# Overlapping the residual and norm boundaries of a two-block transformer kernel with the products on both sides, and moving two gate columns ahead of the attention

## What is computed

```python
# block 1
h = rmsnorm(x, g_pre_mix)
q, k, v, g, u, sv, a_ret, a_sgu = split(h @ w_in)
merged = sigmoid(a_ret) * retention(q, k, v, g) + sigmoid(a_sgu) * spatial_gating(u, sv)
x = x + rmsnorm(merged @ w_out, g_post_mix)                  # out1
h2 = rmsnorm(x, g_pre_ffn)                                   # read by up1
x = x + rmsnorm(conv_gated_mlp(h2, w_up, w_down), g_post_ffn)  # down1
# block 2
h = rmsnorm(x, attn_norm)                                    # h3, read by kv_iq
a_q, a_k, a_v, i_q, i_k, i_w, b_q, b_k, b_v, g_a, g_b = split(h @ w_in_2)
o_a = attention_on_the_128_best_keys(a_q, a_k, a_v, index(i_q, i_k, i_w))
o_b = sliding_window_attention(b_q, b_k, b_v, sinks)
mix = sigmoid(g_a) * (o_a @ w_branch_a) + sigmoid(g_b) * (o_b @ w_branch_b)
x = x + mix @ w_out_2                                        # out2
h2 = rmsnorm(x, mlp_norm)                                    # h4, read by up2
x = x + square(relu(h2 @ w_up_2)) @ w_down_2                 # down2
return rmsnorm(x, final_norm)
```

## Time and profile before

| | us |
|---|---|
| median of three runs | 1676.07 |
| profiled execution | 1677.33 |
| span of its instructions | 1675.5 |
| PE busy | 1620.2 |
| POOL busy | 799.6 |
| DVE busy | 774.1 |
| ACT busy | 491.4 |

### The profile page before, as it was taken

One profiled execution on the slowest core, in us unless ns is written; L12 is line 12 of the kernel. 1 busy time (PEld: TensorE's weight loads), 2 busy tenths in 40 slices (PEclk: granted clock), 3 DMA queues, 4 the chain that ended last, 5 costly groups with the idle time before them and its releaser, 6 DMA issues.

```text
span 1675.5 us, 19583 instructions
## 1 busy us (share of the span) xinstructions
PE 1620.2 (97%) x7556; PEld 1339.4 (80%) x7556; DVE 774.1 (46%) x1076; ACT 491.4 (29%) x735; POOL 799.6 (48%) x304
## 2 busy tenths in 40 slices
PE   7999999999998999999998999979999899999998
PEld 5887788888887888888886887867878788888886
DVE  6701588800555666664005488954452632013202
ACT  3012211200003434333123244245542343123312
POOL 5874287777876444444446003411135444434442
PEclk9999999999999999999998999989999999999999
DMA  5332033332233233332221322210022132232221
GB/s 201 101 126 75 3 105 101 101 101 84 92 101 101 76 101 100 99 90 93 95 101 59 99 79 72 80 51 26 26 76 101 52 99 101 101 101 95 89 97 72
DMA packets 123280, 147.47 MB, mean 88 GB/s; under 512 B 5142, under 2 KB 98374, under 8 KB 123206
## 3 DMA queue, kind: packets, MB, share of 16 engines
q1 hardware_dynamic: 121622, 141.90, 26.2%
q10 hardware_dynamic: 1584, 4.52, 0.8%
HBM read 144.31 MB, written 2.10 MB: 87 GB/s over the span
## 4 chain that ended last, share of the span: by engine, by line
PE 87%; DVE 7%; POOL 3%; issue 1%; ACT 1%; DMA 0%; SPq 0%; DVEq 0%; POOLq 0%; ACTq 0%
PE ps L582 26%; PE ps L583 26%; PE ps L584 26%; PE ps L691 2%; DVE work L1649 2%; PE ps L921 2%; PE ps L761 2%; DVE top L1646 2%; PE ps L907 2%; POOL w_lo L526 1%; DVE h_rows L1340 1%; POOL w_hi L517 1%; PE ps L818 1%; PE ps L749 1%; DMA raw<-in_w_in 0%
## 5 line engine op out<-in xcount | busy, mean ns | idle before, releaser
L526 POOL TENSOR_TENSOR w_lo<-raw,w_hi 128x1024 fp32r<-128x1024 f32 (+1 forms) x246 | 617.8, 2533 | 694.4 <-ACT w_hi L965 690.9
L582 PE MATMUL ps<-hT_hi,w_hi 128*128 128x512 f32 (+1 forms) x960 | 371.4, 387 | 1.0 <-DVE hT_lo L1351 0.5
L584 PE MATMUL ps<-hT_hi,w_lo 128*128 128x512 f32 (+1 forms) x960 | 368.2, 384 | 0.0
L583 PE MATMUL ps<-hT_lo,w_hi 128*128 128x512 f32 (+1 forms) x960 | 368.2, 384 | 0.0
L517 POOL TENSOR_TENSOR w_hi<-raw,cells 128x2048 fp32r<-128x2048 f32 x45 | 168.2, 3739 | 158.9 <-PE ps L582 158.9
L965 ACT ACTIVATE w_hi<-raw 128x2048 fp32r<-128x2048 f32 (+1 forms) x85 | 161.0, 1895 | 247.9 <-PE ps L582 246.2
L582 PEld LDWEIGHTS ps<-hT_hi,w_hi 128*128 128x128 f32 x960 | 181.9, 189 | 36.8 <-POOL w_lo L526 1.4
L584 PEld LDWEIGHTS ps<-hT_hi,w_lo 128*128 128x128 f32 x960 | 181.7, 189 | 35.4
L583 PEld LDWEIGHTS ps<-hT_lo,w_hi 128*128 128x128 f32 x960 | 181.8, 189 | 34.3 <-issue 0.2
L583 PE MATMUL ps<-w_lo,f_hi 128*128 128x512 f32 x432 | 170.2, 394 | 0.0
L582 PE MATMUL ps<-w_hi,f_hi 128*128 128x512 f32 x432 | 169.3, 392 | 0.0
(11 more groups left out here) (258 smaller groups left out, 2128.7 us busy)
## 6 DMA issues: line engine op xcount, KB each, us to landing
raw<-in_w_in SPq DMA_DIRECT2D x86, 512.0 KB, 4.6
raw<-in_w_up SPq DMA_DIRECT2D x76, 512.0 KB, 4.5
raw<-in_w_down SPq DMA_DIRECT2D x54, 512.0 KB, 4.1
raw<-in_w_out SPq DMA_DIRECT2D x16, 512.0 KB, 4.1
raw<-in_w_ret_o SPq DMA_DIRECT2D x8, 512.0 KB, 4.5
raw<-in_w_sgu_o SPq DMA_DIRECT2D x8, 512.0 KB, 4.4
x<-in_x SPq DMA_DIRECT2D x4, 512.0 KB, 7.5
raw<-in_w_branch_b SPq DMA_DIRECT2D x4, 512.0 KB, 4.4
```

The costliest lines, as they stand in the source:

```text
L526: nc.gpsimd.tensor_tensor(w_lo[:, s, c], raw[:, s, c], w_hi[:, s, c].bitcast(f32), ALU.subtract).then_inc(unit_split, 1)
L582: first = nc.tensor.matmul(dst, a_hi, b_hi, start=start, stop=False)
L583: nc.tensor.matmul(dst, a_hi, b_lo, start=False, stop=False)
L584: return first, nc.tensor.matmul(dst, a_lo, b_hi, start=False, stop=stop)
```

## The change

1. **Joint last two units.** In out1, down1, out2 and down2_1 the last two units are worked together, tile by tile (`last_two_L`): each tile gets its 4 x 3 x 2 matmuls of both units and is then complete. After the first half of tiles 2 and 3 PE transposes tiles 0 and 1 of the next `h_rows`.
2. **Next stage.** `first_two_T` takes the place of `first_T`: the first two units (four columns) are worked for the first 256 tokens, then for the rest; tile 2 is transposed ahead of the second column and tile 3 ahead of the fourth. kv_iq works both its units tile by tile, tiles 2 and 3 transposed after its tiles 0 and 1. No keep-warm transposes there.
3. **Slots.** The first unit of each joint pair and the second unit of each next stage have spare slots in memory that is free then. `FREE` says which unit must have started before a hi is written.
4. **Who splits.** From out1 on ACT writes every hi. DVE writes the lo of the first two units after each boundary, ahead of the boundary's steps. POOL adds nothing to `x` any more; DVE adds all four tiles. `STEPS` is A0 B0 A1 C0 B1 A2 C1 B2 A3 C2 B3 C3.
5. **Tickets** are waited for in the new order in which PE completes them (`ORDER`).
6. **Attention.** `GA_IN` is 6: two more gate columns ahead of the attention, 8 parts instead of 16 inside it, at steps 2, 6, ... 30. `index_score(2)` and `(3)` run inside `select(1)`, after its rounds 4 and 10.
7. ACT's loop over up2 is written out instead of looped.

```diff
-GA_IN = KT // 2
-PARTS = [2 + 2 * n for n in range(16)] + [46 + 3 * n // 2 for n in range(16)]
+GA_IN = 6
+GA_PARTS = 4 * (KT - GA_IN)
+PARTS = [2 + 4 * n for n in range(GA_PARTS)] + [46 + 3 * n // 2 for n in range(16)]
...
-GIVEN = [0, *range(U0["up1"] + 2, U0["kv_iq"]), *range(U0["iq_ik"], U0["up2_0"]), *range(U0["up2_0"] + 2, N_UNITS)]
+GIVEN = [0, *range(U0["out1"], N_UNITS)]
+JOINT = {phase: U0[phase] + n - 2 for phase, n in (("out1", 4), ("down1", FB // 2), ("out2", 4), ("down2_1", 8))}
+NEXT = {"out1": "up1", "down1": "kv_iq", "out2": "up2_0"}
+def slot_tables():
+    slot, free = {u: u % 2 for u in range(N_UNITS)}, {u: u for u in range(N_UNITS)}
+    for phase, u in JOINT.items():
+        slot[u], slot[u + 1] = (phase, 0), u % 2
+        free[u], free[u + 1] = u - 1, u
+        if phase in NEXT:
+            slot[u + 2], slot[u + 3] = (u + 1) % 2, (phase, 1)
+            free[u + 2], free[u + 3], free[u + 4] = u + 1, u + 1, u + 3
+    return slot, free
...
+def completion_order():
+    order = list(range(N_TICKETS))
+    for phase, h in (("out1", "h2"), ("down1", "h3"), ("out2", "h4")):
+        o, h, k = T0[phase], T0[h], T0["kv_iq"]
+        after = [o, o + 1, o + 2, o + 3, o + 4, h, h + 1, o + 5, o + 6, h + 2, h + 3, o + 7]
+        if phase == "down1":
+            after += [k, h + 4, h + 5, k + 1, h + 6, h + 7, k + 2, k + 3]
+        for n, t in enumerate(after):
+            order[t] = o + n
+    return order
...
+            def first_two_T(u, t, phase):
                 for half in range(2):
                     for tt in (2 * half, 2 * half + 1):
                         await_h(phase, tt)
                     tok = slice(half * S // 2, (half + 1) * S // 2)
-                    for c in range(2):
+                    for c in range(4):
+                        hi, lo = weights(u + c // 2, KT, 256, wait=half == 0 and c % 2 == 0)
                         if half == 0:
-                            if c == 1:
-                                for tt in (2, 3):
-                                    h_transposes(phase, tt)
+                            if c % 2:
+                                h_transposes(phase, 2 + c // 2)
                             claim(t + c)
...
+            def last_two_L(u, t, k0, l_hi, l_lo, ready, phase):
+                both = [weights(u + j, 2, D, wait=j == 1) for j in range(2)]
+                for kk in range(4):
+                    ready(k0 + kk)
+                for tt in range(NT):
+                    tok = slice(tt * P, (tt + 1) * P)
+                    for half in range(2):
+                        cc = slice(half * 512, half * 512 + 512)
+                        for kk in range(4):
+                            hi, lo = both[kk // 2]
+                            first, last = three(bank(t + 2 * tt + half), l_hi[:, k0 + kk, tok], l_lo[:, k0 + kk, tok],
+                                                hi[:, kk % 2, cc], lo[:, kk % 2, cc], False, kk == 3)
+                            if tt == 0 and half == 0 and kk % 2 == 0:
+                                first.then_inc(unit_started, 1)
+                        last.then_inc(psum_ready, 1)
+                        if phase and half == 0 and tt >= 2:
+                            h_transposes(phase, tt - 2)
...
+            for u in range(JOINT["out1"], U0["up1"] + 2):
+                give_hi(u, started=True)
             boundary("norm", T0["out1"], T0["h2"])
+            give_hi(U0["up1"] + 2, started=True)
...
+            low(U0["up1"])
+            low(U0["up1"] + 1)
             boundary("norm", T0["out1"], T0["h2"], 0, 1)
...
-            for tt in range(1, NT):
-                select(tt)
+            select(1, between={4: 2, 10: 3})
+            select(2)
+            select(3)
```

More of the change, by code:

```diff
@@ L330, in two_blocks @@
         rms_made = sem("rms_made")
-        x_updated = sem("x_updated")
         x_added = sem("x_added")
@@ L551, in _ @@
             split(1)
-            split_all(2, U0["up1"] + 1)
-            boundary(T0["out1"])
-            split(U0["up1"] + 1, last=T0["h2"] - 1)
-            split_all(U0["up1"] + 2, U0["kv_iq"])
-            split(U0["kv_iq"])
-            boundary(T0["down1"])
-            split(U0["kv_iq"] + 1, last=T0["h3"] - 1)
-            pool.wait_ge(unit_split, 2 * (U0["kv_iq"] + 2))
+            split_all(2, U0["out1"])
+            for u in range(U0["out1"], U0["up1"]):
+                split(u)
+            split_all(U0["up1"] + 2, JOINT["down1"])
+            for u in range(JOINT["down1"], U0["kv_iq"]):
+                split(u)
+            await_psum(pool, T0["h3"] - 1)
             zeroed = Count(pool, pads_zeroed)
@@ L565, in _ @@
             zeroed.wait()
-            split_all(U0["g_b"] + 2, U0["up2_0"])
-            split_all(U0["up2_0"], U0["up2_0"] + 2)
-            split_all(U0["up2_0"] + 2, N_UNITS)
+            split_all(U0["g_b"] + 2, U0["out2"])
+            for u in range(U0["out2"], U0["up2_0"]):
+                split(u)
+            split_all(U0["up2_0"] + 2, JOINT["down2_1"])
+            for u in range(JOINT["down2_1"], N_UNITS):
+                split(u)
         @block.tensor
@@ L822, in gb_column @@
                 column(U0["g_b"] + c // 2, G_B[c], KT, 256, c % 2, hT_hi, hT_lo)
-            wide("kv_iq", after="h3")
+            both = []
+            for tt in range(NT):
+                await_h("h3", tt)
+                if tt == 0:
+                    both = [weights(U0["kv_iq"] + h, 4, 512) for h in range(2)]
+                t = T0["kv_iq"] + tt
+                claim(t)
+                tok = slice(tt * P, (tt + 1) * P)
+                for kk in range(KT):
+                    hi, lo = both[kk // 4]
+                    first, last = three(bank(t), hT_hi[:, kk, tok], hT_lo[:, kk, tok], hi[:, kk % 4, :],
+                                        lo[:, kk % 4, :], kk == 0, kk == KT - 1)
+                    if tt == 0 and kk % 4 == 0:
+                        first.then_inc(unit_started, 1)
+                last.then_inc(psum_ready, 1)
+                if tt < 2:
+                    h_transposes("h3", tt + 2)
             wide("iq_ik", IB_W)
@@ L973, in boundary @@
                 step.up(nc.scalar.activation(sq[:, 1:2], eps, ACT.Sqrt))
-                for which, tt in STEPS:
+                for which, tt in steps(kind):
                     tok = slice(tt * P, (tt + 1) * P)
@@ L1118, in _ @@
                 up_unit(j)
-            for u in range(U0["down1"] + 2, U0["kv_iq"]):
+            for u in range(U0["down1"] + 2, U0["kv_iq"] + 2):
                 give_hi(u, started=True)
```

149 lines of the change are left out of this document (82 added, 67 removed).

## The result

The changed kernel took 1632.21 us, the median of four runs (1631.12 to 1632.53), beside 1676.26 for the kernel before on the same chip: a ratio of 0.9735 with a 95% interval of 0.9723 to 0.9747, 44.1 us less. The forecast was 1633.0. The total is right to 0.8 us; of its two parts one is right and one is not, and a third thing, which the forecast didn't have, fills the gap.

What follows compares the result with a forecast made beforehand. PE, busy 97% of the span, bounds the kernel, so only its waits and slow-clock stretches can be won. Boundaries 34.6 plus attention 8.3 give 42.9 us, 1676.07 to 1633.0; own range 1630 to 1636.

Steps and rivals of the forecast that it cites:

- Boundaries: out1 to up1, down1 to kv_iq, out2 to up2_0: gains 12.2, 13.7 and 10.2 us, less 3 x 0.5 stall: 34.6 us.
- T+5.9: Start of ACT's square for tile 0, 5.9 us after the joint product's start T; tile 0 is complete at T+5.6.
- Rival A: Late chain to `h_rows` stalls PE inside the joint product: 4.5 us more, 1637.5; chance 0.17.
- First eight steps: Attention's start, 21.62 us before: falls to 10.0 without the 9.6 us bubble, 11.6 gained; 0.3 lost to DVE.
- DVE free at 1100.9: Before the attention: DVE done about when PE arrives (1101.0, old clock), a tie; 0.3 us taken, up to 4.
- gain of 4.3 us: Index scores 2 and 3 inside select(1) fill DVE's 3.91 us wait and some 0.4 more.
- Steps 8 to 32: Attention, 46.16 us before: 6 parts instead of 12 gain 8.2 us, less 1.5 for latency they had covered.
- Rival B: Attention becomes latency-bound, waits for `probs` and `probs_T` take 6 of 8.2 us: 4.5 more, 1637.5; chance 0.12.
- extra part at step 32: Attention: one more part gone at step 32, 1.2 us gained.
- Moved cells: Shifted buffer addresses, listed as free: no time gained or lost.
- Rival C: The joint product's second unit is late at the boundaries: 6 us more, 1639; chance 0.05.
- D: Slower than before: units of up1 and up2 each wait 1.5 us for weight splitting, 51 us, 1684; chance 0.02.

Runs made afterwards that it cites:

- after_back64: The changed kernel with the region that holds the stage operands (oT, yT, mT, f) starting 64 bytes lower, as in the kernel before: 1637.88 us.
- scores_plain: The changed kernel with index scores 2 and 3 ahead of the mask again, not inside the first selection: 1631.99 us.
- table_first: The changed kernel with the Sqrt table load ahead of ACT's hi copies at each of the three boundaries instead of behind them: 1630.28 us.
- scores_late: The changed kernel with index score 3 placed later in the first selection, after its last but one round instead of after the eleventh: 1630.78 us.

## Why the prediction was right, and where not

- **Boundaries, 34.6 us forecast, 33.5 measured.** The steps held: PE's waits for `h_rows` below 3 us, no keep-warm rows, clock 1.00 throughout, `h_rows` at 1.28 us for every tile. `h_rows` of 3.18 is gone, and POOL is idle from 491 to 532. POOL's memsets after h3 (883.60 to 885.86 in the changed kernel) ran beside the `h_rows` at 884.05, which took 1.29 us: an instruction that only writes did not stretch it, as forecast. From the joint start to the first unit of full width were 50.27, 47.97 and 48.70 us, where 48.9, 47.3 and 48.9 were forecast. At out1 the waits named in the rows are 1.45 us against the 0.5 taken; with 48.9 + 1.45 - 0.64 for the spacing, 0.56 are left that have no row of their own. The step that was mis-sized is the start of the chain: the square was put at T+5.9 and came at T+7.1, because the second unit's hi waited for its load (1.32 us, the DMA) and the table load stood behind it. The forecast had seen that load "just where A0 starts" and put 0 to 0.2 us on it; taking it away removed both waits.
- **Rival A** (4.5 us more) didn't come; the named waits at the three boundaries are 2.1 us, nearer to the 1.5 taken than to its 6.
- **First eight steps, 11.3 us forecast (11.6 less 0.3), 9.15 measured.** The step that failed is "DVE free at 1100.9"; it was 1105.5 by the same clock. Its gain of 4.3 us assumed that the scores take the same time wherever they stand. They fell on a POOL low. Measured, the gain is 0.1 (3.91 of wait less 3.85). PE waited 2.26 us instead of 0.3, and the clock, taken as restored, cost about 1.25; against that some 1.1 us of the stretch came out better than forecast, and were not traced.
- **Steps 8 to 32, 6.7 us forecast, 5.16 measured.** Six parts of 1.37 us were removed (8.2) and 3.0 came back, not 1.5. PE's idle time in the stretch rose from 1.56 us (46.16 - 44.60) to 3.58 (41.00 - 37.42), and cutting the same parts finer takes it to 0.83 (38.05 - 37.22) and the stretch down by 2.95. The comparison of busy times that the forecast used (ACT 1.0, DVE 0.8, PE 1.2 us a step) only says that no engine is over its load. The loss is latency: the chain logits, `probs`, transposes, `probs_T`, values runs over three engines, and where no product stands between, PE waits: 0.98 us at 1093.87, 0.98 at 1107.73 and 1.01 at 1121.62, once in eight steps, and less between. **Rival B** (6 lost) names the mechanism, at twice its size.
- **The extra part at step 32:** 0.78 measured, 1.2 forecast.
- **Spacing, nothing forecast, 7.1 measured.** "Moved cells" was listed under free. The forecast had both values in front of it, 0.227 and 0.233, and took them as properties of the products. It didn't ask why one 512-column matmul should cost 3% more than another.
- **Rival C and D:** no new wait for weights: PE's waits for POOL's lows are 1.9 us in three, 2.0 before.

So that the total was right to 0.8 us is in part luck: 4.1 us too much in the attention and 1.1 at the boundaries stand against 7.1 that the forecast had not counted. The span was off by 2.1 (1632.6 forecast, 1630.5 measured). The medians come closer because the profiled execution before lay 1.1 us above its median of 1676.26 and the one after only 0.3 above its own.

## What to carry to other kernels

When an instruction is moved, look at what the other engines do at its new place: here DVE instructions with two SBUF inputs that began while a GpSimd low was running took about three to four times as long (0.75 and 2.7 us, 1.22 and 3.37, 0.69 and 2.89), and moving one of them once more mostly moved the bill; taking the GpSimd work away there was what paid. When two equal matmul streams show different spacings, compare where their operands start before anything else: distances of a multiple of 512 bytes are the ones that these runs show to be clean. And a filler that hides latency worked here by how often it stood there: the same 48 matmuls in twice as many parts took 2.95 us off.

## What the runs showed of the hardware

- In this kernel 512-column matmuls in a dense stream come every 227 ns where stationary and moving operand start at a multiple of 512 bytes from each other, and with `oT`, `yT` and `mT` every 233 ns where the distance is 64 bytes off it (y_ret: 43.52 and 44.80 us for 192); 128 off costs too (22.19 against 21.76 us for 96 in out2, with `m_lo` alone off). In the products with `f` it was less, 98.88 against 97.92 us for the first nine units of down1 (229 ns in the mean).
- The granted clock was 0.86 over the 12.5 us of the first eight steps, with one wait of 2.26 us among them, in the profiled execution of the changed kernel, and 1.00 in those of three others with a wait of 2.24 or 2.25 us there (`after_back64`, `scores_plain`, `table_first`).
- A DVE `TENSOR_SCALAR` with a single SBUF input was stretched as well, 2.37 us for 256 columns beside a POOL low in `scores_late` where it takes 0.29 in `scores_plain`.
- The one that began first was not stretched: in `scores_late` the scan at 1052.41 took 1.21 us, and the half of a POOL low that began beside it at 1052.60 took 3.22 us instead of 2.4; in the changed kernel POOL began first (1053.53, 2.39 us) and the scan at 1053.64 took 3.37.
